# Feed-forward input of a decoder trunk: seven block products per chunk in place of eight

## The reference, cut to what matters

```python
u  = x * (1 + scale(c)) + shift(c)             # x: (520, 1024)
gu = u @ w_ffn_in[l]                           # (1024, 2 * 2816): gate columns, then up columns
h  = silu(gu[:, :2816]) * gu[:, 2816:]
y  = h @ w_ffn_out[l]                          # (2816, 1024)
x  = layer_norm(ALPHA * x + (1 + gate(c)) * y)
```

## Time and profile before

| what | value |
|---|---|
| median of 3 runs | 1520.35 us (1518.74 to 1520.53) |
| profiled execution, first to last instruction | 1520.7 us |
| TensorE busy | 1411.2 us (93%) |
| VectorE busy | 789.2 us (52%) |
| ScalarE busy | 533.7 us (35%) |
| GpSimd busy | 324.1 us (21%) |

### The profile page before, as it was taken

One profiled execution on the slowest core, in us unless ns is written; L12 is line 12 of the kernel. 1 busy time (PEld: TensorE's weight loads), 2 busy tenths in 40 slices (PEclk: granted clock), 3 DMA queues, 4 the chain that ended last, 5 costly groups with the idle time before them and its releaser, 6 DMA issues.

```text
span 1520.7 us, 29446 instructions
## 1 busy us (share of the span) xinstructions
PE 1411.2 (93%) x12244; PEld 1350.3 (89%) x12244; DVE 789.2 (52%) x1183; ACT 533.7 (35%) x760; POOL 324.1 (21%) x303
## 2 busy tenths in 40 slices
PE   4999987889898999999999999997989999999996
PEld 4899976656697999999999889997979999999995
DVE  4533258764657532333324788897674333333346
ACT  1311152334432432113223446883443321232224
POOL 2000031122054300000003537363641000000054
PEclk8899998889998999999999999998999999999999
DMA  9632287668630332343322312222603224432211
GB/s 312 216 110 57 84 282 247 228 230 290 214 106 7 84 84 67 91 135 84 85 66 87 110 42 80 88 70 55 184 1 111 76 66 122 111 84 76 67 39 57
DMA packets 213503, 175.06 MB, mean 115 GB/s; under 512 B 9079, under 2 KB 183932, under 8 KB 213252
## 3 DMA queue, kind: packets, MB, share of 16 engines
q1 hardware_dynamic: 208448, 160.13, 34.3%
q0 software_dynamic: 4800, 13.23, 2.6%
q10 hardware_dynamic: 140, 0.09, 0.0%
HBM read 167.87 MB, written 5.63 MB: 114 GB/s over the span
## 4 chain that ended last, share of the span: by engine, by line
PE 53%; DVE 12%; ACT 3%; issue 1%; POOL 0%; DVEq 0%; ACTq 0%; POOLq 0%
PE ps L2764 44%; PE ps L2793 4%; PE ps L2773 4%; DVE gn L2204 2%; DVE wlo L1990 2%; DVE UL L2211 1%; DVE xc L2322 1%; DVE rstd L2177 1%; ACT whi L1179 1%; DVE xc L2357 1%; DVE xc L2356 1%; DVE qT L2342 0%; DVE tv L2169 0%; ACT xT L1253 0%; DVE xT L2154 0%
## 5 line engine op out<-in xcount | busy, mean ns | idle before, releaser
L2764 PE MATMUL ps<-UH,whi 128*128 128x260 f32 x1840 | 371.8, 283 | 9.4 <-DVE wlo L1990 9.4
L2764 PE MATMUL ps<-UH,wlo 128*128 128x260 f32 x1840 | 371.2, 283 | 0.0
L2764 PE MATMUL ps<-UL,whi 128*128 128x260 f32 x1840 | 370.7, 283 | 0.0
L1179 ACT ACTIVATE whi<-raw 128x2048 fp32r<-128x2048 f32 (+3 forms) x104 | 178.0, 1712 | 441.0 <-PE ps L2764 388.6
L2764 PEld LDWEIGHTS ps<-UH,whi 128*128 128x128 f32 x1840 | 284.3, 189 | 11.2 <-DVE wlo L1990 8.5
L2764 PEld LDWEIGHTS ps<-UH,wlo 128*128 128x128 f32 x1840 | 284.2, 189 | 0.0
L2764 PEld LDWEIGHTS ps<-UL,whi 128*128 128x128 f32 x1840 | 283.4, 189 | 0.0
L1990 DVE TENSOR_TENSOR wlo<-raw,whi 128x2048 fp32r<-128x2048 f32 (+3 forms) x104 | 224.9, 2162 | 80.8 <-ACT whi L1179 79.0
L2258 DVE TENSOR_TENSOR hb<-ps,silb 128x520 f32<-128x520 f32 x44 | 30.8, 699 | 268.0 <-PE ps L2764 247.9
L830 POOL COPY accS<-xT 128x520 f32<-128x520 f32 x4 | 2.5, 621 | 622.2 <-DVE xT L2136 622.2
L2764 PE MATMUL ps<-HH,whi 128*128 128x260 f32 x484 | 97.4, 283 | 0.0
(11 more groups left out here) (510 smaller groups left out, 2586.2 us busy)
## 6 DMA issues: line engine op xcount, KB each, us to landing
raw<-in_w_ada SPq DMA_DIRECT2D x96, 512.0 KB, 6.7
raw<-in_w_ffn_in SPq DMA_DIRECT2D x88, 512.0 KB, 5.1
raw<-in_w_in_even SPq DMA_DIRECT2D x24, 512.0 KB, 4.8
raw<-in_w_ffn_out SPq DMA_DIRECT2D x32, 384.0 KB, 4.0
raw<-in_w_ffn_out SPq DMA_DIRECT2D x32, 320.0 KB, 3.4
raw<-in_w_in_odd SPq DMA_DIRECT2D x20, 512.0 KB, 4.5
raw<-in_w_out_odd SPq DMA_DIRECT2D x16, 320.0 KB, 3.7
page<-in_cache_k POOLq DMA_DIRECT2D x16, 256.0 KB, 4.7
```

The costliest lines, as they stand in the source:

```text
L1179: ins = nc.scalar.activation(whi[w % 2][:, 0:f], raw[c % NRAW][:, 0:f], ACT.Identity)
L2764: ins = T.matmul(ps(g)[:, hf, 0:HT], wt(k, m), x[:, k, hf], start=(k == 0 and wt is wh and x is xh), stop=(k == s.k - 1 and wt is wl_))
```

## The change

In 40 of the 44 chunks (all but the first two of fi00 and of fi10) the product is computed as a 2 x 2 block product with seven multiplications. The contraction (tiles 0 to 3 and 4 to 7), the columns (gate and up) and the tokens (first and second half) are each cut in two. A block product is 12 matmuls of 260 columns: four contraction tiles and three part products.

For every chunk four sums of weight blocks are made by GpSimd, two of them in place in `raw`. Each of the seven weight blocks (128x512) is then rounded and split apart (`hi7`, `lo7`). One chunk fills both pairs: blocks 0 to 3 lie in the first, blocks 4 to 6 in the second, and the last quarter of the second `whi` holds `wsum`. A block is overwritten when TensorE has used the same block of the chunk before. The four token sums are made once a layer by GpSimd and split by ScalarE and VectorE, while the first two chunks run.

Three products are read out of PSUM on the way by ScalarE (`copy_product`) and three additions are made by VectorE (`add12`, `add22`, `add11`) before Silu and the multiplication. Silu now reads SBUF. The eight multiplications that keep the tokens move between the weight sums, one per chunk (chunks 3 to 10).

```diff
+            r = raw[c % NRAW][:].rearrange("p (k g m) -> p k g m", k=8, g=2)
+            a11, a12, a21, a22 = r[:, 0:4, 0], r[:, 4:8, 0], r[:, 0:4, 1], r[:, 4:8, 1]
+            return (a11, wsum[:], a11, wsum[:], a21, a12, a22)[b]          # seven_source(c, b)
...
+            if before in seven_index and b < 5:                            # block_free(eng, c, b)
+                eng.wait_ge(product_filled, 5 * seven_index[before] + b + 1)
...
+            def weight_sum(n, part):                                       # GpSimd
+                if part == 0:
+                    pool.wait_ge(raw_loaded[n % NRAW], 32 * (n // NRAW + 1))
+                    if holder[n][1] not in seven_index:
+                        slot_free(pool, n, 1)
+                    if i >= 1:
+                        pool.wait_ge(seven_lo, 7 * i - 3)
+                    ins = pool.tensor_tensor(wsum[:], a21, a22, ALU.add)
+                elif part == 1:
+                    ins = pool.tensor_tensor(a21, a11, a21, ALU.subtract)
+                elif part == 2:
+                    pool.wait_ge(seven_lo, 7 * i + 1)
+                    ins = pool.tensor_tensor(a11, wsum[:], a11, ALU.subtract)
+                else:
+                    pool.wait_ge(seven_lo, 7 * i + 2)
+                    ins = pool.tensor_tensor(wsum[:], a12, a11, ALU.subtract)
...
+            def hi7(c, b):                                                 # ScalarE
+                block_free(act, c, b)
+                if 1 <= b <= 4:
+                    act.wait_ge(wsum_ready, 4 * i + (1, 3, 4, 2)[b - 1])
+                nc.scalar.activation(seven_block(b)[0], seven_source(c, b), ACT.Identity).then_inc(seven_hi, 1)
...
+            def seven_products(s, c, it=None, tokens_new=None):            # TensorE
+                for b in range(7):
+                    if b in (2, 3, 4):
+                        pe.wait_ge(copied, 3 * i + b - 1 + later(6))
+                    if b == 6:
+                        pe.wait_ge(u3_used, i + 1 + later(2))
+                    pe.wait_ge(seven_lo, 7 * i + b + 1 + later(14))
...
-                    gemm(f"fi{l}{hf}", UH, UL, ulo_ready, 16 * (2 * l + 1))
+                    ffn_in(l, hf)
```

More of the change, by code:

```diff
@@ L250, in trunk @@
             place[s.c0 + s.n - 3 + i] = where
-    pair_chunks = [c for c in split_chunks if c not in place]
-    pair_index = {c: i for i, c in enumerate(pair_chunks)}
+    slot_of, holder, held = {}, {}, [None, None]
+    turn_of = 0
+    for c in range(n_chunks):
+        if c in seven_index:
+            holder[c], held, turn_of = tuple(held), [c, c], 0
+        elif c in split_index and c not in place:
+            if c == st["oinx"].c0:
+                turn_of = 0
+            slot_of[c], holder[c] = turn_of, held[turn_of]
+            held[turn_of] = c
+            turn_of = 1 - turn_of
     def chunk_last_use(c):
@@ L1319, in ffn @@
                     s = st[f"fi{l}{hf}"]
[L1320 to L1335, removed]
-                        nc.scalar.activation(HH[:, c], hb[c % 2][:], ACT.Identity).then_inc(hhi_ready, 1)
-                        settled(act, hhi_ready)
@@ L1339, in ffn @@
+                    high_h(s, s.n - 1, k0 + s.n - 1)
+                    hi(f0 + 1)
                     s = st[f"fo{l}{hf}"]
@@ L2268, in ffn @@
-                    lo(s.c0 + s.n + 1)
+                    k0 = (2 * l + hf) * KH
+                    ch = s.chunks
+                    f0 = s.c0 + s.n
+                    first = 0
+                    if hf == 0:
+                        if l == 0:
+                            lo7(ch[2], 0)
+                        gated_h(s, 0, k0)
+                        if l == 1:
+                            lo7(ch[2], 0)
+                        lo7(ch[2], 1)
+                        token_low(l, 0)
+                        low_h(s, 0, k0)
+                        gated_h(s, 1, k0 + 1)
+                        token_low(l, 1)
+                        lo7(ch[2], 2)
+                        low_h(s, 1, k0 + 1)
+                        lo7(ch[2], 3)
+                        token_low(l, 2)
+                        lo7(ch[2], 4)
+                        lo7(ch[2], 5)
+                        lo7(ch[2], 6)
+                        token_low(l, 3)
+                        add12(s, 2)
+                        add22(s, 2)
+                        lo7(ch[3], 0)
+                        lo7(ch[3], 1)
+                        add11(s, 2)
+                        for b in range(2, 6):
+                            lo7(ch[3], b)
+                        gated_sums(s, 2, k0 + 2)
+                        lo7(ch[3], 6)
+                        first = 3
@@ new lines, in ffn @@
+                    for c in range(first, s.n):
+                        k = k0 + c
+                        n = ch[c + 1] if c + 1 < s.n else None
+                        if n is not None:
+                            lo7(n, 0)
+                        if c > 0:
+                            low_h(s, c - 1, k - 1)
+                        if n is not None:
+                            lo7(n, 1)
+                            lo7(n, 2)
+                        add12(s, c)
+                        add22(s, c)
+                        if n is not None:
+                            lo7(n, 3)
+                            lo7(n, 4)
+                        else:
+                            lo(f0)
+                        add11(s, c)
+                        if n is not None:
+                            lo7(n, 5)
+                        gated_sums(s, c, k)
+                        if n is not None:
+                            lo7(n, 6)
```

365 lines of the change are left out of this document (329 added, 36 removed).

## The result

The changed kernel takes 1620.53 us (median of four runs, 1617.79 to 1621.86) against 1520.32 before: a ratio of 1.0659 (95% interval 1.0644 to 1.0674). It is 6.6% slower; the prediction said 1627, and its profiled execution spans 1615.8 us.

A forecast was written before the change was run, and what follows sets the result against it. TensorE alone bounds the input stages before; after, a round through ScalarE, VectorE and GpSimd does. 1520.7 + 50 - 2 + 16 + 15 + 25 + 2 = 1626.7, so 1627 us, 8-in-10 range 1556 to 1675.

The forecast's parts named there:

- The steady chunk: 30 of the 40 changed chunks: a round of 13.2 us from Silu to Silu against 11.53 before, +50 us.
- the round without meetings: Steady chunk, lower bound if VectorE and GpSimd never wait for each other: 11.2 us, -10 us in total.
- The meeting at block 5: Steady chunk: VectorE's low part of block 5 partly waits for a GpSimd sum, 0.27 us.
- The hold of 0.98: VectorE instructions with two SBUF operands beside GpSimd: each meeting delays VectorE by 0.77 to 0.98 us, 0.98 taken.
- the 1645 of that estimate: Total by the skill's whole-instruction lock: 0.3 us more per meeting, two meetings in 30 chunks, about +18 us.
- The first chunk of fi01: First chunk of fi01 and fi11: 19.4 us against 11.53, for sums in series and late copies, +16 us for both.
- Third and fourth chunk: In fi00 and fi10, waits for token and weight sums: +15 us in fi00, +25 us in fi10.
- the clock that falls in the gaps: Rival: TensorE's clock drops to 0.66 in steady chunks with gaps, +63 us, about 1690 us; chance 0.11.
- a clock below 1.00 in fi01: Sign in fi01 that was to show the prediction wrong: TensorE's granted clock under 1.00 there.
- The LayerNorm round: Ahead of the input stages: sums meet VectorE's `UL` chain, a `wlo` wait goes; +3 us layer 0, -1 layer 1.
- Meetings free: Rival for the input stages: GpSimd sums let VectorE through, round 11.2 us, total about 1555 us; chance 0.14.
- TensorE the bound: Rival for the input stages: the round falls under 10.09 us, total 1463 to 1508 us; chance 0.05.

The follow-up runs named there:

- e1: The changed kernel with its four weight sums per chunk cut to one column of each contraction tile, waits and order kept: 1520.15 us.
- e3: The changed kernel with each weight sum replaced by two constant GpSimd writes that read nothing from SBUF: 1545.3 us.
- e9: The changed kernel with blocks 3 to 6 of the first chunk of fi01 and fi11 rounded between its copies, not ahead of them: 1622.48 us.
- e6: The changed kernel with ScalarE and VectorE reordered in the steady chunks and weight sums of one column: 1494.81 us.
- e4: The changed kernel with the multiplication with Silu put ahead of low part 5 of the next chunk on VectorE: 1605.19 us.
- e2: The changed kernel with its four weight sums working on half of their columns (256 of 512 elements per partition): 1562.65 us.

## Why the prediction was right

**What bounds.** As said: TensorE bounds before, a round of ScalarE, VectorE and GpSimd after. TensorE is busy 80% of fi01, where the text had 76% for the steady chunk (a row counts a matmul's whole way through the array).

**The steady chunk**, 13.2 predicted, 13.1 measured; TensorE's waits are 1.29 and 1.15 at blocks 3 and 6, where 1.5 and 1.3 were worked out. The prediction gives 11.2 for the round without meetings, but its own terms add up to 11.57 + 1.35 - 2 x 0.99 = 10.9, and 10.8 was measured in e1: the steps and hand-overs together were right, the bound was added up wrongly. The meeting at block 5 costs 0.43 where 0.27 was taken. The hold of 0.98, from `HL` in the earlier trace rows, came back as 0.99 in the low parts. TensorE spent 10.55 us on the last chunk of fi01 and 11.0 on that of fi00; 11.0 was predicted (10.8 in the line on fi01).

The Trainium skill ("SBUF — State Buffer", sections "SBUF: two separate sides" and "Who interferes with whom") has the lock held for the whole instruction, and none with a GpSimd instruction that only writes. The second agrees with e3 (0.69 beside a write). The first holds but for the 0.14 us at the end, yet in the two long meetings of a round a low part never came at the very start of a sum's own work, so what it lost was 0.99 us and not the 1.28 of the estimate by that page; the 1645 of that estimate is 25 us too long.

**The first chunk of fi01**, 19.4 predicted, 19.3 measured. Block 2 starts 9.35 us into the stage (702.17 - 692.82), 9.3 predicted. At block 6 TensorE waits 1.08 where 2.5 was worked out: behind the wait of 4.00 us the granted clock was 0.68 (702.1 to 707.0), so the products in between took longer and less was left to wait for. The sum was right and its reason was half right: e9 shows that the copies behind the four roundings are not what counts.

**Third and fourth chunk.** 20.1 and 18.3 us in fi00, 30.1 and 18.3 in fi10 were predicted. By the starts of TensorE's first matmuls they took 19.9 (501.13 to 521.07) and 19.5 us (to 540.55) in fi00, 30.2 (1179.88 to 1210.05) and 18.2 us (to 1228.25) in fi10. The pieces differ. At block 4 of the third chunk of fi00 TensorE waited 1.07 where 3.3 was worked out, as its waits show:

```profile
...
515.92 0.36 PE L3302 MATMUL ps<-tH,whi 128*128 128x260 f32 x1 [1.07 <-issue]
...
527.41 0.38 PE L3302 MATMUL ps<-tH,whi 128*128 128x260 f32 x1 [3.30 <-ACT silb L1518]
...
```

The clock took most of the difference (stretches, columns as in the earlier trace rows):

```profile
...
510.00:515.00 5.00, 4.85 (x24) 4.64 (x24) 4.83 (x6) 3.41 (x7) 2.85 (x2) 0.59 0.00 0
...
540.00:580.00 40.00, 33.79 (x265) 32.04 (x265) 30.77 (x47) 23.49 (x40) 23.49 (x16) 1.00 0.29 79
...
```

Behind the wait of 5.65 us the granted clock was 0.59 (of the levels 2.4 and 1.2 GHz nearly the lower), 24 matmuls took 4.85 us in place of 2.9, and the low parts were ready meanwhile. This rival, the clock that falls in the gaps, was real behind the long waits of fi00, fi01 and fi10; by the prediction's own sign (a clock below 1.00 in fi01, where the row says 0.99) it was right in the first chunk. That the total came out all the same is in part luck: the prediction put this clock at nothing, and the slower matmuls mostly filled time in which TensorE would have waited anyway. Not all of it did: the fourth chunk of fi00 took 1.2 us more than predicted, at clocks of 0.56 and 0.67 (527.0 to 533.0 and 533.0 to 540.5), and the fifth, with 12.4, gave 0.8 back; that the clock made the 1.2 is inferred. In the steady chunks, with waits of 1.2 us, the clock stayed at 1.00 as the row of 7.30 in the earlier trace rows had suggested.

**The stages.** The prediction's terms make fi00 128.6, fi01 and fi11 149.0 and fi10 138.6 us long; measured are 128.7, 148.1, 147.9 and 138.3. So 1627 is near for the reasons given, stage by stage.

**Two rows misread**, without effect on the sum. In the earlier trace rows the roundings at 672.43 and 683.93 are those of the second and third chunk of fi01, whose first was rounded at 664.54; and the 66 matmuls of the earlier trace rows stand at the end of fo01, not in the attention part.

**The LayerNorm round.** +3 and -1 predicted; from the first mean of the round before fi00 to the third chunk of fi00 44.6 us before and 48.0 after, and in layer 1 from the last part of fo01 (its matmuls with weights in `UH`) to the third chunk 301.3 and 299.5: +3.4 and -1.8.

**What the sum missed.** 101.5 + 3.4 - 1.8 = 103.1 us, where the prediction's terms add up to 106; the two profiled executions differ by 95.1. Most of the rest lies ahead of fi00, in work that the change doesn't touch: that first mean is computed at 460.51 us in the execution before and at 453.13 in that after. In the nine experiments it lies between 454.98 and 459.52. Neither execution is typical of its kernel: 1520.7 is 4.1 us above the median span of the 27 executions of the kernel before that stand beside e1 to e9 (1516.6, from 1513.0 to 1523.6), and 1615.8 is the shortest span of the changed kernel's four (median 1618.8). These medians differ by 102.2 (the times of the result by 100.2), so most of the 8 us belong to these two executions and not to the change. The granted clock dips at other places in the attention part (320 to 330 us: 0.66 in the earlier trace rows, 0.85 after); whether that makes executions differ was not tried and stays open.

**The rivals.** Meetings free (1555; 1548 with the round of 10.9) is e3, 1545; TensorE the bound (1463 to 1508) is e6, 1495. Both were priced well and needed something that the change doesn't have.

## What to carry to other kernels

When an engine at 100% gets less work, write down the round of the other engines in their program order, from one instruction back to the same one, with lengths from the trace; the longest such round is the new pitch, whatever the busy shares say. A GpSimd instruction that reads SBUF is not free because GpSimd idles: price each VectorE instruction with two SBUF operands that can run beside it. And a wait that is removed at one place is worth only what the next wait leaves, as e9 shows beside e4.

## What was not expected of the hardware

What a meeting costs VectorE goes by how much of the GpSimd sum is still to come: in every meeting of the rounds looked at the low part was done 0.69 us after a moment 0.14 us before the sum's end. A low part that started 0.16 us behind a sum of 512 elements (1.29 us) lost 0.99, one that started 0.73 behind such a sum lost 0.43 (block 5, 727.01 behind 726.28), and one 0.15 behind a sum of 256 (0.73 us, in e2) lost 0.43. Beside a sum of 4 (e1) it lost nothing. So short sums cost less than in proportion. GpSimd waits as VectorE does: in e1 a sum of 4 elements lasts 0.21 us, but 0.66 where `HL` started 0.1 us ahead of it (702.03 above):

```profile
...
702.14 0.66 POOL L959 TENSOR_TENSOR raw<-wsum,raw 128x4 f32<-128x4 f32 x1 [5.69 <-DVE wlo L2252]
703.60 0.21 POOL L962 TENSOR_TENSOR wsum<-raw 128x4 f32<-128x4 f32 x1 [0.80 <-DVE wlo L2252]
...
```
